# A two-block network on one Trainium2 core: order of the spectrum's halves, place of a weight split, width of the squared sums

## What is computed

```python
def _l2norm(t):
    return t * lax.rsqrt(jnp.sum(t * t, axis=-1, keepdims=True) + 1e-6)

# _deltanet_group: five taps over the sequence, then unit-length queries and keys
qkv = jax.nn.silu(_dwconv(jnp.concatenate([q, k, v], axis=-1), conv_w))
q, k, v = jnp.split(qkv, [DN_KEY, 2 * DN_KEY], axis=-1)
q = _l2norm(to_heads(q, DN_DK)) * (DN_DK ** -0.5)
k = _l2norm(to_heads(k, DN_DK))

# _hyena_group: two long convolutions, each by way of a spectrum
for o, gate in enumerate((x1, x2)):
    zz = gate * (_fft_conv(zz, kspec[:, o]) + skip[o] * zz)

def _fft_conv(z, kspec):
    l = z.shape[1]
    zs = jnp.fft.rfft(z, n=2 * l, axis=1)
    return jnp.fft.irfft(zs * kspec[None], n=2 * l, axis=1)[:, :l]
```

## Time and profile before

| what | us |
|---|---|
| median of 3 runs (lowest to highest) | 3929.32 (3927.19 to 3929.78) |
| the profiled execution, its own time | 3931.74 |
| its span in the profile | 3929.9 |
| TensorE busy in the span | 3796.0 |
| DVE, ACT, POOL busy | 2039.7, 1093.2, 69.1 |
| mean granted TensorE clock | 0.98 of full |

### The profile page before, as it was taken

The page is one execution under the profiler, slowest core; times in us unless marked ns, Lnnn a source line. Parts: engine busy times, 40 slices in busy tenths (PEclk is TensorE's granted clock), DMA queues, the critical chain, the costliest instruction groups (busy, mean ns, idle before and its releaser), DMA issues.

```text
span 3929.9 us, 43107 instructions
## 1 busy us (share of the span) xinstructions
PE 3796.0 (97%) x17694; PEld 3086.3 (79%) x17694; DVE 2039.7 (52%) x2512; ACT 1093.2 (28%) x1193; POOL 69.1 (2%) x81
## 2 busy tenths in 40 slices
PE   9999999989999999999999999999999999999997
PEld 8878888756788878888777678888888776878886
DVE  5564434553654435434664764434443756575442
ACT  3242222342422222222333222222222242322221
POOL 0000000000000000000010000000000102000000
PEclk9999999998999999999999999999999999999998
DMA  3212222100222222223302222222222313112221
GB/s 135 102 70 96 96 94 100 59 32 36 82 95 98 97 81 95 97 91 123 106 27 81 86 75 96 96 100 94 96 94 99 129 53 97 65 65 96 96 91 70
DMA packets 66788, 343.01 MB, mean 87 GB/s; under 512 B 23524, under 2 KB 23524, under 8 KB 30816
## 3 DMA queue, kind: packets, MB, share of 16 engines
q1 hardware_dynamic: 60864, 303.19, 21.8%
q0 software_dynamic: 5792, 37.92, 2.6%
HBM read 324.31 MB, written 16.78 MB: 87 GB/s over the span
## 4 chain that ended last, share of the span: by engine, by line
PE 86%; DVE 9%; ACT 2%; issue 1%; DMA 1%; SPq 0%; DVEq 0%; ACTq 0%
PE ACC L986 25%; PE ACC L988 25%; PE ACC L987 25%; PE ACC L1617 1%; PE ACC L1351 1%; DVE BX L2867 1%; DVE BT L2865 1%; PE ACC L1331 1%; PE MIX L1263 1%; DVE WL L2274 0%; DVE PT L3054 0%; DVE PT L3056 0%; DMA RAW<-wall 0%; PE MIX L1160 0%; PE ACC L1649 0%
## 5 line engine op out<-in xcount | busy, mean ns | idle before, releaser
L986 PE MATMUL ACC<-HH,WH 128*128 128x512 f32 (+1 forms) x3322 | 1308.2, 394 | 28.6 <-issue 15.3
L988 PE MATMUL ACC<-HH,WL 128*128 128x512 f32 (+1 forms) x3322 | 1291.0, 389 | 0.0
L987 PE MATMUL ACC<-HL,WH 128*128 128x512 f32 (+1 forms) x3322 | 1290.9, 389 | 0.0
L2274 DVE TENSOR_TENSOR WL<-RAW,WH 128x2048 fp32r<-128x2048 f32 x292 | 668.3, 2289 | 481.2 <-ACT WH L1785 480.7
L986 PEld LDWEIGHTS ACC<-HH,WH 128*128 128x128 f32 x3322 | 627.2, 189 | 179.0 <-issue 35.9
L987 PEld LDWEIGHTS ACC<-HL,WH 128*128 128x128 f32 x3322 | 627.2, 189 | 131.3 <-issue 5.3
L988 PEld LDWEIGHTS ACC<-HH,WL 128*128 128x128 f32 x3322 | 626.7, 189 | 129.6
L1785 ACT ACTIVATE WH<-RAW 128x2048 fp32r<-128x2048 f32 x292 | 556.6, 1907 | 559.7 <-PE ACC L988 554.6
L2369 DVE TENSOR_TENSOR SG<-ACC,RS 128x512 f32<-128x512 f32 x132 | 91.3, 692 | 628.6 <-PE ACC L988 628.4
L986 PE MATMUL ACC<-HIDH,WH 128*128 128x512 f32 x1056 | 410.8, 389 | 0.0
L987 PE MATMUL ACC<-HIDL,WH 128*128 128x512 f32 x1056 | 410.8, 389 | 0.0
(11 more groups left out here) (503 smaller groups left out, 3033.4 us busy)
## 6 DMA issues: line engine op xcount, KB each, us to landing
RAW<-wall SPq DMA_DIRECT2D x261, 1024.0 KB, 4.7
RAW<-wall SPq DMA_DIRECT2D x24, 768.0 KB, 4.1
KR<-spectra POOLq DMA_DIRECT2D x4, 2048.0 KB, 9.0
x_kept<-X POOLq DMA_DIRECT2D x2, 2048.0 KB, 7.1
FWK<-mats POOLq DMA_DIRECT2D x4, 1024.0 KB, 5.4
spectra<-SQ POOLq DMA_DIRECT2D x8, 512.0 KB, 3.0
spectra<-T POOLq DMA_DIRECT2D x8, 512.0 KB, 3.8
X<-x_kept POOLq DMA_DIRECT2D x2, 2048.0 KB, 14.1
```

The source lines that it names most:

```text
L986: pe.matmul(out_ap, wh, hh, start=first, stop=False)
L987: pe.matmul(out_ap, wh, hl, start=False, stop=False)
L988: return pe.matmul(out_ap, wl, hh, start=False, stop=last)
L2274: v.tensor_tensor(WL[n % 2][:], RAW[n % 2][:], WH[n % 2][:], ALU.subtract).then_inc(w_lo, 1)
```

## The change

- **Semaphores.** Seven of the memory branch become three (one for each engine that signals), and nine of the cell's become two, each counted up. `hy_so` is new. Who waits for which instruction stays.
- **Spectrum.** TensorE makes the two odd banks of an fc first and signals them (`hy_so`), then the two even ones (`hy_sp`). ACT copies the odd banks, now in two instructions of 512 elements, when `hy_so` says so; DVE's `combine` waits for the copy and for `hy_sp`. In `next_spectrum` the odd times are transposed and copied first too, with a signal for each half.
- **Five-tap projection.** ACT splits unit n + 2 at the head of each block's turn but the last; DVE splits it behind the read of ACC and ahead of the taps.
- **Sums of squares of q and k.** The moving operand is all of ONES, 128 columns for 1; the output of each product covers 128 columns, of which the first is kept and the others are overwritten or not read.

```diff
@@ pe_prep, step 2
-                            mm = pe.matmul(MIX[:, 2, 4 * m + tc:4 * m + tc + 1], src[:, tc * P:tc * P + P], ONES[:, 0:1],
+                            mm = pe.matmul(MIX[:, 2, 4 * m + tc:4 * m + tc + P], src[:, tc * P:tc * P + P], ONES[:],
                                            start=True, stop=True)
@@ pe_delta
-                def signal_spectrum(fc, cs):
+                def signal_spectrum(fc, p, css):
                     bank = (ACC, MIX)[fc]
-                    for p in range(2):
+                    for cs in css:
                         for kc in range(2):
...
-                signal_spectrum(0, 0)
+                signal_spectrum(0, 1, (0, 1)).then_inc(hy_so, 1)
                 pe.wait_ge(dn_oc, 4 * L + 4)
                 head_scales(1, MIX[:, 0:2])
-                signal_spectrum(0, 1).then_inc(hy_sp, 1)
-                signal_spectrum(1, 1)
+                signal_spectrum(0, 0, (0, 1)).then_inc(hy_sp, 1)
+                signal_spectrum(1, 1, (1,))
                 pe.wait_ge(t_ready, st.h0 + 4)
-                signal_spectrum(1, 0).then_inc(hy_sp, 1)
+                signal_spectrum(1, 1, (0,)).then_inc(hy_so, 1)
+                signal_spectrum(1, 0, (0, 1)).then_inc(hy_sp, 1)
@@ pe_hyena, next_spectrum
-                        for q in range(4):
+                        for q in (2, 3, 0, 1):
                             first = q // 2 + 2 * P * (q % 2)
                             mm = pe.transpose(MIX[:, q, m * P:m * P + P], HY[:, m, first:first + 2 * P - 1:2], ident)
-                    mm.then_inc(hy_zt, 2)
+                            if m == 3 and q % 2:
+                                mm.then_inc(hy_zt, 1)
                     for fc, bank in ((0, ACC), (1, MIX)):
-                        for p in range(2):
-                            pe.wait_ge(hy_ztc, 4 * L + 4 if fc else 4 * L + 3 + p)
+                        for p in (1, 0):
+                            pe.wait_ge(hy_ztc, 4 * L + 4 if fc else 4 * L + 4 - p)
...
-                        mm.then_inc(hy_sp, 1)
+                            mm.then_inc((hy_sp, hy_so)[p], 1)
@@ act_linear
+                                if st.out == "conv5":
+                                    if i * 2 + j < st.nb - 1:
+                                        split_hi(n + 2, add, i)
+                                    continue
                                 if st.opens and isinstance(i, int) and i == 0:
@@ act_hyena
                     if o:
-                        act.wait_ge(hy_zt, 4 * L + 4)
-                        for half in range(2):
+                        for half in (1, 0):
+                            act.wait_ge(hy_zt, 4 * L + 4 - half)
                             act.activation(ZT[:, 2 * half:2 * half + 2, :], MIX[:, 2 * half:2 * half + 2, :], ACT.Copy).then_inc(hy_ztc, 1)
                     for fc, bank in ((0, ACC), (1, MIX)):
-                        act.wait_ge(hy_sp, 2 * n + fc + 1)
+                        act.wait_ge(hy_so, 2 * n + fc + 1)
                         if 2 * n + fc:
                             act.wait_ge(hy_spd, 2 * n + fc)
-                        act.activation(T[:], bank[:, 1:4:2, :], ACT.Copy).then_inc(hy_odd, 1)
+                        for cs in range(2):
+                            odd = act.activation(T[:, cs, :], bank[:, 2 * cs + 1, :], ACT.Copy)
+                        odd.then_inc(hy_odd, 1)
@@ dve_linear
-                                if st.opens and isinstance(i, int) and i == 0:
+                                if st.out == "conv5" or st.opens and isinstance(i, int) and i == 0:
                                     continue
...
                             v.tensor_tensor(CVT[:, j], two, scale2, ALU.mult).then_inc(block_done, 1)
+                            if st.out == "conv5" and 0 < i * 2 + j < st.nb - 1:
+                                n, add = unit_of(st, i, j)
+                                split_lo(n + 2, add, i)
                             v.wait_ge(cv_center, cv)
@@ dve_hyena, combine
                     v.wait_ge(hy_odd, 2 * n + fc + 1)
+                    v.wait_ge(hy_sp, 2 * n + fc + 1)
                     v.tensor_tensor(ZS[:, fc, 0:4:2, :], bank[:, 0:4:2, :], T[:], ALU.add)
@@ one of sixteen renamed hand-overs
-                pe.wait_ge(mem_diag, 1)
+                pe.wait_ge(mem_dve, 2)
```

More of the change, by code:

```diff
@@ L595, in build @@
         xs_out = sem("xs_out")
[L596 to L602, removed]
+        mem_act = sem("mem_act")
+        mem_dve = sem("mem_dve")
+        mem_pe = sem("mem_pe")
         out_done = sem("out_done")
@@ L617, in build @@
         ma_out = sem("ma_out")
-        ml_turned = sem("ml_turned")
-        ml_abs = sem("ml_abs")
+        ml_columns = sem("ml_columns")
+        ml_gates = sem("ml_gates")
         ml_log = sem("ml_log")
[L621 to L626, removed]
         ml_em = sem("ml_em")
@@ L704, in build @@
         kf_k = sem("kf_k")
+        hy_so = sem("hy_so")
         hy_sp = sem("hy_sp")
@@ L1188, in memory_sums @@
             def memory_sums():
-                pe.wait_ge(mem_added, 1)
+                pe.wait_ge(mem_dve, 1)
                 for c in range(KD // 2):
@@ L1193, in memory_sums @@
                                        start=(c == 0 and mc == 0), stop=(c == KD // 2 - 1), skip_group_check=True)
-                mm.then_inc(mem_summed, 1)
+                mm.then_inc(mem_pe, 1)
             def memory_scale():
-                pe.wait_ge(mem_diag, 1)
-                pe.matmul(MIX[:, 1, 0:M_MEM], ONES[:], DIAG[:, 0:M_MEM], start=True, stop=True).then_inc(mem_scale, 1)
+                pe.wait_ge(mem_dve, 2)
+                pe.matmul(MIX[:, 1, 0:M_MEM], ONES[:], DIAG[:, 0:M_MEM], start=True, stop=True).then_inc(mem_pe, 1)
             def pe_even(st):
                 pe.wait_ge(mem_landed, 32)
-                pe.wait_ge(mem_scaled, 1)
+                pe.wait_ge(mem_dve, 3)
                 for at, g in enumerate(EVEN_ORDER):
@@ L1689, in pe_mlstm @@
                     mm = pe.transpose(MIX[:, 0, 8 * tc:8 * tc + 8], OZ[32:40, 5, tc * P:tc * P + P], ident[32:40, 32:40])
-                mm.then_inc(ml_turned, 1)
+                mm.then_inc(ml_columns, 1)
                 keep_clock(ACC[:, 0, :], 16)
-                pe.wait_ge(ml_ls, 1)
+                pe.wait_ge(ml_gates, 2)
                 for j in range(TC):
@@ L1696, in pe_mlstm @@
                                        start=(i == 0), stop=(i == j))
-                mm.then_inc(ml_f, 1)
-                pe.wait_ge(ml_af, 1)
+                mm.then_inc(ml_columns, 1)
+                pe.wait_ge(ml_gates, 3)
                 for tc in range(TC):
@@ L1701, in pe_mlstm @@
                     mm = pe.transpose(MIX[0:4, 3, tc * P:tc * P + P], LF[:, tc, :], ident)
-                mm.then_inc(ml_rows, 1)
+                mm.then_inc(ml_columns, 1)
                 keep_clock(ACC[:, 0, :], 10)
-                pe.wait_ge(ml_rowsm, 1)
+                pe.wait_ge(ml_gates, 4)
                 for tc in range(TC):
                     mm = pe.transpose(MIX[:, 0, 4 * tc:4 * tc + 4], LR[:, 3, tc * P:tc * P + P], ident[0:4, 0:4])
-                mm.then_inc(ml_mcol, 1)
+                mm.then_inc(ml_columns, 1)
                 pe.wait_ge(ml_em, 1)
@@ L1986, in memory_squares @@
                     a = act.activation(MSQ[:, 4 * half:4 * half + 4, :], MEM[:, 4 * half:4 * half + 4, :], ACT.Square)
-                a.then_inc(mem_squared, 1)
+                a.then_inc(mem_act, 1)
             def memory_root():
-                act.wait_ge(mem_summed, 1)
-                act.activation(RN[:, 0, 0:MC], MIX[:, 0, 0:MC], ACT.Sqrt, bias=EPSC[:], scale=1.0 / D).then_inc(mem_root, 1)
+                act.wait_ge(mem_pe, 1)
+                act.activation(RN[:, 0, 0:MC], MIX[:, 0, 0:MC], ACT.Sqrt, bias=EPSC[:], scale=1.0 / D).then_inc(mem_act, 1)
             def act_silu_qk(st):
@@ L2220, in act_mlstm @@
             def act_mlstm(st):
[L2221 removed]
+                act.wait_ge(ml_gates, 1)
                 act.activation(LT[:, 1, :], LT[:, 0, :], ACT.Exp, scale=-1.0).then_inc(act_step, 1)
@@ L2390, in period @@
                             if i == 3:
-                                v.wait_ge(mem_scale, 1)
+                                v.wait_ge(mem_pe, 2)
                                 v.tensor_tensor(MEM[:], MEM[:], MIX[:, 1, 0:M_MEM].unsqueeze(1).to_broadcast([P, KD, M_MEM]), ALU.mult)\
-                                    .then_inc(mem_scaled, 1)
-                                v.wait_ge(mem_scaled, 1)
+                                    .then_inc(mem_dve, 1)
+                                v.wait_ge(mem_dve, 3)
                         elif st.out == "even":
@@ L2403, in period @@
                             if i == 1:
-                                v.wait_ge(mem_squared, 1)
-                                v.tensor_tensor(MSQ[:, 0:4, :], MSQ[:, 0:4, :], MSQ[:, 4:8, :], ALU.add).then_inc(mem_added, 1)
```

(2 more changed lines are left out.)

23 lines of the change are left out of this document (11 added, 12 removed).

## The result

| what | before | after |
|---|---|---|
| median (lowest to highest), us | 3929.55 (3927.19 to 3932.55), 4 runs | 3906.01 (3898.46 to 3907.99), 4 runs |
| ratio, with its 95% interval | | 0.9936 [0.9919, 0.9953] |
| profiled execution, its span | 3931.74, 3929.9 | 3905.41, 3903.6 |

Faster, as forecast, and inside the range, but by 23.5 us between the medians (26.3 between the two spans) where 33.0 were forecast. The interval of the ratio allows 18 to 32. The same kernel measured again with the experiments gave a median of 3908.92; over all its ten runs the median is 3907.3, against 3928.8 over the 48 runs of the kernel before in all comparisons: 21.5 less. So the change is worth 21 to 26 us, and something between 7 and 12 is missing.

What follows compares the result with a forecast made beforehand. TensorE was taken to bound the kernel (86% of the chain, DVE 9%). Five-tap projection 16.2, sums of squares 12.8 and spectra 4.0 sum to 33.0 less: 3929.3 to 3896.3 us, range 3889 to 3910.

Steps and rivals of the forecast that it cites:

- Sums of squares: Sums for q and k: 64 records take 7.0, following work runs at full clock; 6.4 a layer, 12.8 us less.
- Spectra: Both convolutions: DVE's combine no longer waits for the late copy of the odd banks; 2.0 a layer, 4.0 us less.
- The 0.7 of the first: First convolution: two copies end at 2203.3, so DVE starts at 2203.35 for 2204.06, 0.7 us sooner.
- Five-tap projection: Early splits remove TensorE's pause at the fourth block and its slow matmuls; 7.8 and 8.4 by layer, 16.2 us less.
- the row shows DVE slowed by 0.6, not stopped: Five-tap projection: a split moved beside POOL's work costs DVE only 0.6 us, so 16.2 stands.
- The alternative of 12: Five-tap projection, far bound: the split waits out POOL, TensorE sees about 2 us per layer; 12 us less for 16.2.
- A chain that can spare 1.1 a block: Five-tap projection: DVE's turn of 9.8 under TensorE's block of 10.95, so 0.6 lost beside POOL is absorbed.
- The sums' gain isn't given back: Rival, between hy2 and the delta stage: a late chain leaves TensorE idle and gives back the gain; 3909 us, chance 0.06.
- 128 columns hold the clock: Rival, sums of squares: 128 columns don't hold the clock and 64 records take 14.3; 3916 us, chance 0.05.
- the pause was the split's: Rival, five-tap projection: the pause is fetching or something else, so 16.2 is lost; 3912.5 us, chance 0.04.
- no load is late: Rival, five-tap projection: an early split waits for a load taking over 17 us, holding up DVE; slower, 3960 us, chance 0.02.
- the changed order of the spectra is worth its 4: Rival, convolutions: the new order does nothing there; 3900 us, chance 0.03.

Runs made afterwards that it cites:

- second experiment: The kernel before with only the sums of squares of queries and keys widened from 1 to 128 columns; 3917.28 us, ratio 0.9967.
- ninth: The changed kernel with 64 columns for 128 in the sums of squares; 3907.66 us in one run.
- third experiment: The kernel before with only the new order of the spectrum and the merged semaphores; 3925.84 us, ratio 0.9990.
- fifth run: The changed kernel measured once more with no edit; 3908.92 us, ratio 0.9943.
- fourth experiment: The changed kernel with POOL's two instructions on the filter's weights held back until the first zg block has been read; 3893.63 us, ratio 0.9904.
- first: The kernel before with only the change's early splits in the five-tap projection; 3916.91 us, ratio 0.9966.
- seventh experiment: The changed kernel with 19 filler products for 8 ahead of the second half of each inverse transform; 3899.61 us, ratio 0.9919.
- tenth: The kernel before with more filler ahead of both halves of the inverse transforms, 25 and 19 for 18 and 8; 3925.25 us, ratio 0.9994.
- sixth: The changed kernel with the second zg block's unit also split early, behind the read of the sixth block; 3893.27 us, ratio 0.9898.

## Why the prediction was right, and where its size was off

**What bounds the kernel.** Right. The time fell by what left TensorE's pauses and slow stretches and DVE's leads, and the chain afterwards has the same shape.

**Sums of squares, 12.8 forecast, 12.6 measured.** Right in each step: 7.30 where 64 x 0.11 = 7.0 stood, the tail and hy2's head at full clock, and a gain that passes on to the end (second experiment: 12.7). That one column is no cheaper than many, as the rows said while the clock was full, holds for 64 too (ninth). The spacing by columns that the prediction set against it from the Trainium skill (TensorE: Matmul & The Clock Gate, section Back-to-back issue gap) is given there for a product by itself; the same section says that it counts too little where each product has a weight load, which is the case here, and 7.25 for 64 columns against 7.30 for 128 shows no such spacing.

**Spectra, 4.0 forecast, 4.2 measured.** Right, in both convolutions and in the third experiment. The 0.7 of the first was 0.8.

**Five-tap projection, 16.2 forecast, 9.0 measured.** The mechanism was right: the pause was the split's, and it went with its slow matmuls. The step that failed is the one on POOL, "the row shows DVE slowed by 0.6, not stopped", from which 16.2 was taken and not 12. The 6.88 of the earlier trace rows are taps beside POOL's second instruction, L979 there. Its first, L976, had fallen on the end of a split, on DVE's read of ACC and on its wait of 1.41 for ACT, and had cost DVE nothing: the split ended first, and POOL took 3.16 for 2.40. With the split moved ahead of the taps DVE has no such wait left, and the first instruction falls on work: on the split in layer 0 (2.0 longer, and the taps behind it 0.8), on the taps in layer 1 (2.7 longer with both instructions). So the chain was 2.8 and 2.7 late, where the prediction had 0.6.

The Trainium skill (SBUF — State Buffer, section SBUF: two separate sides) has DVE with two SBUF inputs and GpSimd exclude each other for a whole instruction. For the split the trace agrees, in both directions: 2.0 more beside an instruction of 2.40 that had started first, and POOL's second instruction takes 4.69 where a split still runs as it starts, 2.78 or 3.10 where none does (the kernel before; layer 1 of the changed one). It doesn't account for the 0.6 that the taps, which also read twice from SBUF, lost beside all of the 2.78. The alternative of 12 that I worked out from the rule was nearer to the 9.0 than 16.2.

Two omissions turned the 12 into 9. "A chain that can spare 1.1 a block" is right as a pace (the reads at 1860.00 and 1869.62 lie 9.62 apart, blocks 10.88), but I counted the spare time as free, and DVE had use for it: the block read at 1860.00 had ended by 1855.90, when ACT's split, which waits for the same end, began. DVE starts 4.1 behind, four turns win back 4 x 1.26 = 5.0, and 0.9 is all that was spare against POOL's 2.8. So the sixth block is read at 1901.30, 1.9 after its end at 1899.4 (1888.54, ACT's fourth split, + 10.88), and the second zg block's unit is late by as much. And I priced that pause as a pause alone, though the earlier trace rows had shown ten slow matmuls behind the old one. With a pause of 2.40 in place of 0.3, and 1.6 for slow matmuls, each layer loses 3.7: 16.2 - 7.4 = 8.8, and 9.0 was measured. Without the slow matmuls it would be the 12.0 of the alternative; the fifth run, which has them in one layer only, lies between, at 10.7. The fourth experiment confirms it from the other side: with POOL moved, the read of the sixth block waits for TensorE (0.48 idle), 67.04 stands where 66.9 was forecast, and the stage is 7.7 + 8.2 = 15.9 shorter than before, for the 16.2 of the forecast. With the other two terms that makes 32.7, against the 33.0 forecast and 36.3 between its medians.

**The rivals.** None came about. The sums' gain isn't given back (second experiment), 128 columns hold the clock (ninth: 64 do too), the pause was the split's (first, fourth), no load is late: the early splits start right behind the read, and the changed order of the spectra is worth its 4. The case that came about, DVE held up by POOL, stood as the far bound of the five-tap term, 12, and the 9.0 lies outside even that. That the whole stayed in the range is owed to the other two terms, which came out at their middle while the range allowed for both to fall short; for this term it was luck.

**What remains.** 25.8 in the stages against 21 to 26 over the runs: the rest is within what untouched stretches vary by. The transforms behind 3.00 of pause are one place of it (seventh experiment), the delta stage another (tenth); I didn't settle which pattern comes in which run, nor why the fourth and sixth kernels fell by 14 where their stages explain 6.9 and 8.5. The copy of T in two halves could be one; but one strided copy over the odd banks would span a bank that TensorE is writing at that time, and it wasn't tried.

## What to carry to other kernels

When an instruction moves, look at every engine that shares memory with its new place, GpSimd's above all, and price the overlap from that instruction's own kind and length, not from a different one that happened to stand beside it before. Price a pause of TensorE with the slow matmuls behind it, which here cost 1.6 behind 2.40 of pause and up to 3 behind 3.00, in some runs and places and not in others. What DVE can take beside GpSimd depends on where it waits: an instruction of GpSimd that was free while DVE waited cost 2 us and more once that wait was filled. And measure parts alone before adding fixes: four different repairs here each reached 0.990, and together no more.

## What was not expected of the hardware

- Behind an idle stretch of the same 3.00 us, the same 32 records took 7.17, about 8.8 or about 10.1, from run to run and place to place; with the pause filled down to 0.55 they always took 7.17.
- Two engines stretch each other: beside POOL's L967 (2.40) a split took 4.30 for 2.28, and POOL's L970, which started while that split ran, took 4.69 for 2.78. Beside the same two instructions eight taps took 8.94 to 9.07 for 6.25, but beside the second one alone only 6.88.
- The granted clock fell while the profile shows TensorE busy without a break: under records of one column with a new weight each it ended at 0.50, under those of 64 and 128 columns it stayed at 1.00, at about the same pitch as one column has while the clock is full.
- A filler that runs at a better clock is a shorter filler: 56 records covered 8.14 in one run and 6.52 in another, and then left TensorE idle for 3.13.
